# Low halves of the weights: one ring of eight units, in place, made by VectorE outside the FFN and by GpSimd inside it

## The reference, cut to what matters

```python
proj = rms_norm(h, ln_pre_mix) @ w_in
f = (jax.nn.silu(f @ w_ffn_gate) * (f @ w_ffn_up)) @ w_ffn_down
```

## Time and profile before

| what | value |
|---|---|
| median of 3 runs | 1151.17 us |
| span of the profiled execution | 1149.0 us (about 2.2 us of the median lie outside it) |
| PE busy | 1029.0 us, 90% |
| DVE busy | 491.8 us, 43% |
| ACT busy | 524.7 us, 46% |
| POOL busy | 710.5 us, 62% |
| weight units | 294, loaded at a mean of 147 GB/s over the span |

### The profile page before, as it was taken

One profiled execution on the slowest core, in us unless ns is written; L12 is line 12 of the kernel. 1 busy time (PEld: TensorE's weight loads), 2 busy tenths in 40 slices (PEclk: granted clock), 3 DMA queues, 4 the chain that ended last, 5 costly groups with the idle time before them and its releaser, 6 DMA issues.

```text
span 1149.0 us, 13563 instructions
## 1 busy us (share of the span) xinstructions
PE 1029.0 (90%) x5316; PEld 870.1 (76%) x5316; DVE 491.8 (43%) x764; ACT 524.7 (46%) x753; POOL 710.5 (62%) x298
## 2 busy tenths in 40 slices
PE   3987999997999799898999999687788789999996
PEld 3976888986888588686888888576667677888885
DVE  4587442497542754682111021744655525111102
ACT  4365545444534344563544345354434445454431
POOL 3765442675442388587787878564365265978782
PEclk9998999998999899899999999898888999999999
DMA  6534332353321466555655657344145243765550
GB/s 227 184 127 122 98 94 72 118 163 124 108 94 57 147 210 206 156 173 161 183 181 172 192 178 265 112 162 130 55 125 148 76 147 111 221 197 169 182 183 37
DMA packets 75831, 168.52 MB, mean 147 GB/s; under 512 B 7316, under 2 KB 12536, under 8 KB 75512
## 3 DMA queue, kind: packets, MB, share of 16 engines
q1 hardware_dynamic: 69968, 156.78, 43.7%
q10 hardware_dynamic: 5800, 10.88, 3.0%
HBM read 166.59 MB, written 1.05 MB: 146 GB/s over the span
## 4 chain that ended last, share of the span: by engine, by line
PE 67%; DVE 21%; ACT 5%; issue 3%; DMA 2%; POOL 1%; ACTq 1%; DVEq 0%
PE L L455 16%; PE L L456 15%; PE L L457 15%; DVE small L1419 5%; DVE small L1410 2%; PE Q L735 2%; PE Q L749 2%; PE L L618 2%; PE L L620 2%; PE L L619 2%; DVE C L1419 2%; POOL w_lo L445 1%; PE Q L539 1%; DVE small L1416 1%; DMA raw<-in_w_in 1%
## 5 line engine op out<-in xcount | busy, mean ns | idle before, releaser
L445 POOL TENSOR_TENSOR w_lo<-raw,w_hi 128x1024 fp32r<-128x1024 f32 x294 | 710.3, 2434 | 416.3 <-ACT w_hi L1000 416.2
L1000 ACT CAST w_hi<-raw 128x1024 fp32r<-128x1024 f32 x294 | 306.8, 1053 | 294.4 <-PE L L457 209.0
L455 PE MATMUL L<-w_hi,uH 128*128 128x512 f32 (+1 forms) x832 | 331.3, 398 | 10.2 <-DVE uL L1410 6.6
L456 PE MATMUL L<-w_lo,uH 128*128 128x512 f32 (+1 forms) x832 | 322.5, 388 | 0.0
L457 PE MATMUL L<-w_hi,uL 128*128 128x512 f32 (+1 forms) x832 | 322.3, 387 | 0.0
L455 PEld LDWEIGHTS L<-w_hi,uH 128*128 128x128 f32 x832 | 160.5, 193 | 42.3 <-DVE uL L1410 8.3
L457 PEld LDWEIGHTS L<-w_hi,uL 128*128 128x128 f32 x832 | 159.6, 192 | 31.8
L456 PEld LDWEIGHTS L<-w_lo,uH 128*128 128x128 f32 x832 | 160.4, 193 | 29.6 <-issue 0.5
L1459 DVE TENSOR_TENSOR tmp<-L,gA 128x512 f32<-128x512 f32 x20 | 13.0, 686 | 151.7 <-ACT tmp L1252 151.7
L455 PE MATMUL L<-w_hi,hH 128*128 128x512 f32 x176 | 70.0, 398 | 1.5 <-DVE hm L1419 1.5
L457 PE MATMUL L<-w_hi,hL 128*128 128x512 f32 x176 | 69.7, 396 | 0.0
(11 more groups left out here) (305 smaller groups left out, 1346.5 us busy)
## 6 DMA issues: line engine op xcount, KB each, us to landing
raw<-in_w_in SPq DMA_DIRECT2D x88, 512.0 KB, 3.4
raw<-in_w_ffn_gate SPq DMA_DIRECT2D x22, 512.0 KB, 3.7
raw<-in_w_ffn_up SPq DMA_DIRECT2D x22, 512.0 KB, 3.6
raw<-in_w_ffn_down SPq DMA_DIRECT2D x22, 512.0 KB, 3.7
raw<-in_w_gate SPq DMA_DIRECT2D x22, 512.0 KB, 4.1
raw<-in_w_up SPq DMA_DIRECT2D x22, 512.0 KB, 3.7
raw<-in_w_down SPq DMA_DIRECT2D x22, 512.0 KB, 3.6
raw<-in_w_xkv SPq DMA_DIRECT2D x16, 512.0 KB, 3.8
```

The costliest lines, as they stand in the source:

```text
L445: nc.gpsimd.tensor_tensor(w_lo[:, n % SPLIT, :], raw[:, n % RAW, :], w_hi[:, n % SPLIT, :].bitcast(F32), ALU.subtract).then_inc(w_lo_there, 1)
L455: mm(dst, sH, wH, start=start, stop=False)
L456: mm(dst, sH, wL, start=False, stop=False)
L1000: copy(w_hi[:, u % SPLIT, :], raw[:, u % RAW, :]).then_inc(w_hi_there, 1)
```

## The change

There is one ring of 8 units. `w_lo` lies on the same bytes as `raw`: the low half is written over the raw unit. So a unit is loaded into slot n mod 8 only when PE has used unit n-8 (`w_used`), ACT casts it when it has landed, and the low half is made by one of two engines. `on_pool` gives POOL the units of the FFN's column steps c = 1 to 5 and the first 18 of the 22 units of the down projection, in both FFNs: 108 units. DVE makes the other 186. Its program has new places for them: at the start of each step that isn't inside another, `lo_up_to(consumed + LOOK)` with LOOK = 5, two units in step `u`, and `fill` inside `inv` and `yb`. DVE waits there for the high half of the unit (`w_hi_there`). PE waits per unit for the engine that makes it. ACT's places are the same, but SPLIT is now 8 in their formulas, so each cast runs two units further ahead than before.

```diff
--- before.py
+++ after.py
@@ -14,6 +14,7 @@
 
 
 from contextlib import ExitStack
+from itertools import accumulate
 
 import numpy as np
 
@@ -43,7 +44,8 @@
 LEVELS = 7
 LAM_INIT = 0.2
 WINDOWS = (2, 4, 8, 16)
-RAW, SPLIT = 4, 6
+SPLIT = 8
+LOOK = 5
 UNIT = 1024
 KB = 1024
 MAGIC = 1.5 * 2.0 ** 23
@@ -206,6 +208,11 @@
     return units
 
 
+def on_pool(step, i):
+
+    return (step[0] == "ffn" and step[2] > 0) or (step[0] == "down" and i < FF // P - 4)
+
+
 def build(nc, a, out, known):
 
     w = {n: (a[n][0] if len(a[n].shape) == 3 else a[n]) for n in
@@ -232,9 +239,9 @@
                 at[0] += -(-size // 32) * 32
             return nc.alloc_sbuf_tensor_at(name, list(shape), dt, offset=offset)
 
-        raw = place("raw", [P, RAW, UNIT])
+        raw = place("raw", [P, SPLIT, UNIT])
+        w_lo = place("w_lo", [P, SPLIT, UNIT], F32R, base)
         w_hi = place("w_hi", [P, SPLIT, UNIT], F32R)
-        w_lo = place("w_lo", [P, SPLIT, UNIT], F32R)
         uH = place("uH", [P, KD, SEQ], F32R)
         uL = place("uL", [P, KD, SEQ], F32R)
         table = place("table", [P, 12 * P + 2 * NT * HD + ROPE2])
@@ -391,8 +398,9 @@
 
 
         tensor_done, scalar_done, vector_done = sem("tensor_done"), sem("scalar_done"), sem("vector_done")
-        w_landed = [sem(f"w_landed{n}") for n in range(RAW)]
-        w_hi_there, w_lo_there, w_used = sem("w_hi_there"), sem("w_lo_there"), sem("w_used")
+        w_landed = [sem(f"w_landed{n}") for n in range(SPLIT)]
+        w_hi_there, w_used = sem("w_hi_there"), sem("w_used")
+        lo_by_pool, lo_by_vector = sem("lo_by_pool"), sem("lo_by_vector")
         PE = Done(tensor_done, known.get("pe"))
         AC = Done(scalar_done, known.get("act"))
         VE = Done(vector_done, known.get("dve"))
@@ -402,6 +410,13 @@
         landed = {n: sem(f"{n}_landed") for n in load_names}
         stored = sem("stored")
 
+        BY_POOL = [on_pool(step, n - FIRST[step]) for n, (step, _) in enumerate(UNITS)]
+        POOL_COUNT = list(accumulate(int(b) for b in BY_POOL))
+
+        def lo_there(n):
+
+            return (lo_by_pool, POOL_COUNT[n]) if BY_POOL[n] else (lo_by_vector, n + 1 - POOL_COUNT[n])
+
         def fed(step, units=None):
 
             return w_used, (LAST[step] + 1 if units is None else FIRST[step] + units)
@@ -426,10 +441,10 @@
                 sp.dma_start(x0[:, t, :], a["x"][0][t * P:(t + 1) * P, :]).then_inc(landed[f"x{t}"], 16)
             sp.dma_start(ln0[:], row(a["ln_pre_mix"][0], D)).then_inc(landed["ln0"], 16)
             for n, (step, src) in enumerate(UNITS):
-                if n >= RAW:
-                    sp.wait_ge(w_lo_there, n - RAW + 1)
-                dst = raw[:, n % RAW, :].rearrange("p (k n) -> p k n", k=src.shape[1])
-                sp.dma_start(dst, src).then_inc(w_landed[n % RAW], 16)
+                if n >= SPLIT:
+                    sp.wait_ge(w_used, n - SPLIT + 1)
+                dst = raw[:, n % SPLIT, :].rearrange("p (k n) -> p k n", k=src.shape[1])
+                sp.dma_start(dst, src).then_inc(w_landed[n % SPLIT], 16)
             for n in range(2 * NT):
                 c, t = n // NT, n % NT
                 cc = slice(c * 512, (c + 1) * 512)
@@ -441,9 +456,10 @@
         @block.gpsimd
         def _(pool):
             for n in range(len(UNITS)):
-                pool.wait_ge(w_hi_there, n + 1)
-                nc.gpsimd.tensor_tensor(w_lo[:, n % SPLIT, :], raw[:, n % RAW, :], w_hi[:, n % SPLIT, :].bitcast(F32),
-                                        ALU.subtract).then_inc(w_lo_there, 1)
+                if BY_POOL[n]:
+                    pool.wait_ge(w_hi_there, n + 1)
+                    nc.gpsimd.tensor_tensor(w_lo[:, n % SPLIT, :], raw[:, n % SPLIT, :], w_hi[:, n % SPLIT, :].bitcast(F32),
+                                            ALU.subtract).then_inc(lo_by_pool, 1)
 
 
         @block.tensor
@@ -465,7 +481,7 @@
 
                 n0 = FIRST[step] if n0 is None else n0
                 per = UNIT // n
-                pe.wait_ge(w_lo_there, n0 + j + 1)
+                pe.wait_ge(*lo_there(n0 + j))
                 wH, wL = unit(n0 + j, per)
                 for i in range(per):
                     k = j * per + i
@@ -485,7 +501,7 @@
 
                 n0 = FIRST[step]
                 turned(step, k)
-                pe.wait_ge(w_lo_there, n0 + k + 1)
+                pe.wait_ge(*lo_there(n0 + k))
                 wH, wL = unit(n0 + k, 2)
                 tile = ROW_ORDER[step][k] if step in ROW_ORDER else k
                 for t in range(NT):
@@ -610,7 +626,7 @@
                             if pair == 0 and k % 2 == 0:
                                 if gr == 0 and part == 0:
                                     pe.wait_ge(*VE(("u",), "lo", k // 2))
-                                pe.wait_ge(w_lo_there, n0 + k // 2 + 1)
+                                pe.wait_ge(*lo_there(n0 + k // 2))
                             wH, wL = unit(n0 + k // 2, 2)
                             for ct in (pair, pair + 2):
                                 bank = L[b0 + ct // 2][:, (ct % 2) * SEQ:(ct % 2 + 1) * SEQ]
@@ -799,7 +815,7 @@
 
                     for k in range(2):
                         n = FIRST[step] + k
-                        pe.wait_ge(w_lo_there, n + 1)
+                        pe.wait_ge(*lo_there(n))
                         wH, wL = unit(n, 2)
                         for t in range(NT):
                             for c in range(2):
@@ -994,10 +1010,8 @@
 
                 while made[0] < min(n, len(UNITS)):
                     u = made[0]
-                    act.wait_ge(w_landed[u % RAW], 16 * (u // RAW + 1))
-                    if u >= SPLIT:
-                        act.wait_ge(w_used, u - SPLIT + 1)
-                    copy(w_hi[:, u % SPLIT, :], raw[:, u % RAW, :]).then_inc(w_hi_there, 1)
+                    act.wait_ge(w_landed[u % SPLIT], 16 * (u // SPLIT + 1))
+                    copy(w_hi[:, u % SPLIT, :], raw[:, u % SPLIT, :]).then_inc(w_hi_there, 1)
                     made[0] += 1
 
             def hi_wide(step, dst, tiles=range(4)):
@@ -1477,8 +1491,29 @@
                     for t in range(NT):
                         vector_next(V.tensor_tensor(hg[:, t, cc], h[:, t, cc], gB[:, cc], ALU.mult), step, "next", t, part)
 
+            made = [0]
+
+            def lo_up_to(n):
+
+                while made[0] < min(n, len(UNITS)):
+                    u = made[0]
+                    if not BY_POOL[u]:
+                        dve.wait_ge(w_hi_there, u + 1)
+                        V.tensor_tensor(w_lo[:, u % SPLIT, :], raw[:, u % SPLIT, :], w_hi[:, u % SPLIT, :].bitcast(F32),
+                                        ALU.subtract).then_inc(lo_by_vector, 1)
+                    made[0] += 1
+
+            def fill(step, i):
+
+                lo_up_to(FIRST[FILLING[step][0]] + i + LOOK)
+
+            consumed = 0
             for step in SCHEDULE:
                 kind = step[0]
+                if step in LAST:
+                    consumed = max(consumed, LAST[step] + 1)
+                if kind != "u" and step not in INSIDE:
+                    lo_up_to(consumed + LOOK)
                 if kind == "u":
                     v(V.memset(rt, 1.0), step, "warm")
                     dve.wait_ge(*AC(step, "ss", 1))
@@ -1490,6 +1525,7 @@
                                                            op0=ALU.mult, op1=ALU.mult), step, "scaled", t)
                     dve.wait_ge(*PE(step, "taps"))
                     v(V.tensor_copy(cw, L[3][:, 0:CONV * 24]))
+                    lo_up_to(2)
                     lo_wide(step, uH, uL)
                     dve.wait_ge(landed["ba"], 16)
                     bv = ba_raw.rearrange("p (k n) -> p k n", k=KD)
@@ -1643,6 +1679,7 @@
                         vector_next(V.tensor_tensor(T[:, t], each(ident, GH), heads(Q[t]), ALU.subtract), step, "T", 0, t)
                     mask(1)
                     for l in range(1, LEVELS):
+                        fill(step, l + 1)
                         if l < LEVELS - 1:
                             dve.wait_ge(*PE(step, "X", l, 1))
                             mask(l + 1)
@@ -1688,6 +1725,7 @@
                         tt(ot, ot, over(rq[:, t * 8:(t + 1) * 8], HD), ALU.mult)
                         tt(ot, ot, each(gnorm, 8), ALU.mult)
                         tt(o[:, t, :], o[:, t, :], z[:, t, :], ALU.mult, step, "y", t)
+                        fill(step, 2 * t + 2)
                     lo_wide(step, uH, uL)
                     dve.wait_ge(landed["mem"], 16)
                     dve.wait_ge(landed["lnm"], 16)
```

## The result

| | median | runs | ratio to before (95%) |
|---|---|---|---|
| before, in the same session | 1151.23 us | 4 | |
| changed kernel | 1198.11 us | 4 (1197.10 to 1198.97) | 1.0412 (1.0397 to 1.0427) |

The change makes the kernel slower by 47 us. The forecast said slower, by 11 us, with a range that ended at 1175: the sign was right and the size was not.

The account below looks back on a forecast made before the run. The prediction took the kernel as bound by PE, with holes that POOL's weight work makes through DVE. 1149.0 - 26.6 + 27.8 + 10.3 = 1160.5 us, with 2.2 outside 1162.7, stated as 1162; range 1138 to 1175.

Parts of the forecast that it names:

- The hole of norm x: PE's wait at the end of xo: cast and squares come late behind the load, so 4.36 us grows by 3.6.
- The mask of inv: Four low halves before inv's first mask, which PE's turning waits for; 0.99 us of hole takes 1.0, cost 3.6 each, twice.
- Unit 217: At xq, made only after next's reciprocal root: PE's wait of 5 us, 4.6 at the cross attention.
- unit 233: At ffn (2, 0), late like the unit at xq: costs 3.6 us with two POOL operations in the way.
- rope2's hole: PE's hole of 8.96 us behind rope2's slow DVE operations closes; gain 8.0 us.
- The faster rival: Batches slip into idle time, loads land in time for ACT, two smaller conditions hold: 1142 us; chance 0.27.
- unit 107: At ffn (1, 0), behind two roots and four e operations: +5.0 us taken, bounds -1.2 and +7.5.
- the term for ACT and the loads: Loads start only at PE's signal, delaying casts and squares at norm x, xkv 0, down 1 and norm mix2: +10.3 us.
- The slower rival: With 8 units as whole stock, loads take 8 us at the six norms: +12, 1174 us; chance 0.18.
- The two sums for VectorE: Gains of 26.6 us from DVE operations freed of POOL; costs of 27.8 us from low halves in DVE's program.
- the eight holes of the earlier trace: PE's idle times ending on DVE or ACT work that carry the argument: together 38 us.
- the batches ahead of conv 2 and of the sums of tok: Two batches of four low halves on DVE, 4.6 to 5 us each, leaving gains of 2.2 in group 1, 0.9 in group 0.

Follow-up runs that it names:

- cast_6_ahead: Changed kernel with ScalarE's casts placed 6 units ahead instead of 8, the ring left at 8 units: 1137.5 us.
- ring_all_pool: Changed kernel with every low half made by GpSimd, the one ring of 8 and casts 8 ahead kept: 1181.1 us.
- old_rings: Changed kernel on the rings of before (4 raw slots, 6 for the halves, casts 6 ahead), low halves split between engines as changed: 1151.9 us.
- quiet_pool: Kernel before with GpSimd's subtraction cut to 64 of each unit's 1024 columns, the other low halves left 0: 1054.3 us.
- quiet_late: quiet_pool with each low half made only when the next unit's high half is there too: 1062.7 us.
- placed: cast_6_ahead with VectorE's low halves moved ahead of what TensorE comes to, and units 0 and 1 given to GpSimd: 1092.7 us.
- placed_8_ahead: placed with ScalarE's casts 8 units ahead instead of 6, nothing else: 1154.7 us.
- pool_cast_6: Changed kernel with every low half made by GpSimd and casts 6 ahead, on the one ring of 8: 1151.2 us.
- placed_2: placed with units 0 and 1 back on VectorE ahead of the taps wait, and the xkv batches behind the next norm's first halves: 1083.4 us.

## Why the prediction was right in sign and wrong in size

**What held.** The sizes read from single rows came out. The hole of norm x was put at 4.36 + 3.6 = 8.0 us and is 7.86. The mask of inv was put 3.6 later and its hole went from 0.99 to 4.52. Unit 217 was to make PE wait 5 us (4.91), unit 233 some 3.6 (3.21). rope2's hole closed. DVE's subtraction takes 1.22 us (1.24 forecast). The faster rival named the deciding point, whether the cast at the end of a product waits for its load, and gave 1142 for the case that it does not, with two smaller conditions. cast_6_ahead took 1137.5, but that nearness is partly luck: one of the conditions, unit 107 at its lower bound, isn't met there (PE waits 11.39 us for it), and at the end of xo a cast still waits 1.64 us for its load, only early enough to hold up nothing.

**The step that failed: the loads.** "Sum 3.6 + 3.0 + 4.0 - 0.3 = 10.3" was the term for ACT and the loads, and "SP waits for one semaphore in place of another, nothing" stood beside it. With the low halves moved, the ring's own part was a gain of 14.4 us and the distance of the casts a loss of 60.6, so the term measures +46.2; with GpSimd making them all it measures +28.9 (ring_all_pool), still nearly three times the forecast. I had seen that a load now starts at PE's signal, and had priced one late cast at four places. But `SPLIT` stands in every place formula of ScalarE, so casts wait for loads all through the program (213 times, against 20 before). Between cast_6_ahead and the changed kernel PE's waits grow in several lists: for w_lo from 38.8 to 52.2 us, for uL from 8.1 to 24.0, for hg from 4.7 to 11.7, for pL from 0.2 to 4.2, for prT from 1.7 to 4.3. The term should have been asked for at each place, beginning with what `SPLIT` going from 6 to 8 does: it takes away the two units of time, 2.7 us each, in which a load of mostly 3.4 to 3.7 us could land. The slower rival had looked at the loads too, by their length. Two long ones do stand in the changed kernel's chain:

```profile
424.90 6.36 DMA raw<-in_w_proj_b
727.80 7.96 DMA raw<-in_w_ple_gate
```

Behind them PE waits 4.24 us for pL (at 433.67) and 6.65 for uL (at 738.09). With casts 6 ahead the same holes are 0.2 and 2.28.

**The two sums for VectorE were each too small by more than three times, and cancelled.** Forecast: -26.6 and +27.8, net +1.2. Measured: net -0.3 (old_rings), but with up to some 90 us of gain (the 98 of quiet_pool less the 8.4 of quiet_late), so with nearly as much of cost. That the net came out is luck. On the gain's side I took the eight holes of the earlier trace rows and left "some two dozen smaller ones as they are"; they weren't: 70 of PE's 120 us of idle time went with GpSimd's work, more than the 39 us that those eight add up to (the forecast has 38), and 26 us of PE's busy time with it. On the cost's side, the batches ahead of conv 2 and of the sums of tok were counted against VectorE's own root only. PE's fill units stand behind them too: 5.69, 4.12 and 6.02 us at units 13, 17 and 21 in group 0, where I had left a gain of 0.9 us (2.55, 4.12 and 5.14 with casts 6 ahead, so 4.0 us of them are the loads' part). I missed the hole of 5.90 us at 902.07, four low halves ahead of the uL of xq: 2.26 us with casts 6 ahead, the places' part, and the rest the loads'.

**Unit 107** was taken at +5.0 us with an upper bound of +7.5. PE's hole there is 12.69 us, 7.0 more than the 5.65 of before. VectorE's timeline of the changed kernel shows why, with GpSimd's beside it:

```profile
528.16 2.43 DVE L1433 SCALAR_TENSOR_TENSOR small<-small 128x2 f32<-128x2 f32 x2
530.63 2.27 DVE L1424 TENSOR_TENSOR small<-small 128x2 f32<-128x2 f32 x1
532.93 4.56 DVE L1433 SCALAR_TENSOR_TENSOR small<-small 128x2 f32<-128x2 f32 x2
...
537.92 3.12 DVE L1433 SCALAR_TENSOR_TENSOR e<-e,small,lnp 128x512 f32<-128x512 f32 x4
541.07 3.50 DVE L1502 TENSOR_TENSOR w_lo<-raw,w_hi 128x1024 fp32r<-128x1024 f32 x3
```

```profile
528.19 9.28 POOL L461 TENSOR_TENSOR w_lo<-raw,w_hi 128x1024 fp32r<-128x1024 f32 x4 [3.17 <-ACT w_hi L1014]
```

Four turns of the root are lost to GpSimd's four subtractions, then GpSimd stands without casts from 537.5 on, and the four e operations are clean at 3.12 us. The Trainium skill (SBUF — State Buffer, "Who interferes with whom") says of VectorE's two-port modes that whoever issues first gets the shared pair of ports for the whole instruction; of an operation with two SBUF inputs, as most of these are, it says that it contends with a GpSimd operation that reads SBUF. The rows agree as to the contention, and they show VectorE losing the turn at each tiny operation while GpSimd has work, the reading that the forecast preferred. On the rings of before (old_rings) GpSimd has only one unit to make there, VectorE loses one turn (2.22 us at 516.80), and the hole is 5.44 us: the longer ring let GpSimd's work in beside the root.

**The clock was in no term.** Behind each wait of several us PE runs a few us at half its clock. Between before and quiet_pool that is 26 us of busy time beside 70 of idle time; between the changed kernel and cast_6_ahead 17 beside 45. The other pairs give the same or more (placed and placed_8_ahead 19 beside 44, pool_cast_6 and ring_all_pool 11 beside 24). So an us of hole was worth some 1.4 to 1.5 us, and I priced every one at its length, gains and losses alike. The Trainium skill (TensorE: Matmul & The Clock Gate, Part 1) says that the half rate is the default state, released by activity, and by that rule a stall costs again behind its end; the rows here agree (0.63 us for a matmul that otherwise takes 0.39, at a granted clock of 0.51).

**What stays open.** The distance of the casts costs 60.6 and 62.0 us where VectorE makes the low halves, and 29.9 where GpSimd does. That VectorE stands still at a late cast with its norms behind it, while GpSimd has nothing behind it, fits, and PE's wait for VectorE's w_lo grows by 13.4 us in the one pair; but no run takes it by itself. How the cost of the low halves in VectorE's program divides between the holes is argued, not measured: the new places gave back 44.8 us, placed_2 9.3 more, of the up to 90. Casts 5 ahead were not tried.

## What to carry to other kernels

This is what the case suggests. When a ring is made longer, look at every formula that holds its length. A place that runs as far ahead as the ring is long meets each buffer at the moment it comes free: keep the consumer's distance shorter than the ring by the time that the load takes. Work moved onto an in-order engine costs by its place: put each piece in an idle time ahead of the moment at which the consumer comes to it, not in a batch at the head of a step. And price a hole of TensorE with the slow stretch behind it.

## What was not expected of the hardware

- GpSimd's subtractions, 710 us of work on an engine that is 1% of the chain that ended last, cost this kernel about 90 us through VectorE's operations on SBUF: quiet_pool with 64 of 1024 columns takes 1054.3 us instead of 1152.2.
- TensorE's busy time for the same 5316 matmuls ran from 1003.0 to 1042.7 us, with the mean granted clock from 0.992 to 0.944. Here the clock follows the holes.
